# Third mixer's inverse in blocks of 32x32 and 64x64 at its two last levels, and its first products by pairs of heads

## The reference

```python
def _rwkv_scan(seqs, s0):
    # S_t = S_(t-1) diag(w_t) - (S_(t-1) kk_t) (kk_t * a_t)^T + v_t k_t^T,  y_t = S_t r_t
    def step(s, inp):
        rt, lwt, kt, vt, kkt, at = inp
        sa = jnp.einsum('bhvk,bhk->bhv', s, kkt)
        s = (s * jnp.exp(lwt)[:, :, None, :] - sa[..., None] * (kkt * at)[:, :, None, :]
             + vt[..., None] * kt[:, :, None, :])
        return s, jnp.einsum('bhvk,bhk->bhv', s, rt)
```

## Time and profile before

| | |
|---|---|
| runs of the kernel | 2309.73 us median of 3 (2306.72 to 2310.21) |
| the profiled execution | 2299.72 us, its span 2298.2 us |
| TensorE busy | 2160.4 us, 94% of the span |
| VectorE, ScalarE, GpSimd busy | 46%, 26%, 20% |
| granted clock of TensorE, mean | 0.972 of full speed |
| the chain that ended last | TensorE 82%, VectorE 6%, ScalarE 4%, DMA 3% |

### The profile page before, as it was taken

One profiled execution on the slowest core, in us unless ns is written; L12 is line 12 of the kernel. 1 busy time (PEld: TensorE's weight loads), 2 busy tenths in 40 slices (PEclk: granted clock), 3 DMA queues, 4 the chain that ended last, 5 costly groups with the idle time before them and its releaser, 6 DMA issues.

```text
span 2298.2 us, 33450 instructions
## 1 busy us (share of the span) xinstructions
PE 2160.4 (94%) x13459; PEld 2058.7 (90%) x13459; DVE 1054.4 (46%) x1540; ACT 604.8 (26%) x799; POOL 459.4 (20%) x463
## 2 busy tenths in 40 slices
PE   5998998899999897999999999999999999999995
PEld 3997887899999786899999999999999999999994
DVE  4051332467575445443433478642222235656654
ACT  3331221523232143112221243010000013333342
POOL 1122112444454331110000276210000010000012
PEclk9999998999999898999999999999999999999997
DMA  4122123412222240110101475131111224111112
GB/s 157 37 57 61 56 68 70 176 57 61 69 77 62 76 165 29 38 47 20 37 19 37 161 254 187 46 114 44 46 46 46 93 106 165 46 46 37 46 46 84
DMA packets 48563, 177.31 MB, mean 77 GB/s; under 512 B 6401, under 2 KB 6753, under 8 KB 48241
## 3 DMA queue, kind: packets, MB, share of 16 engines
q1 hardware_dynamic: 23040, 85.65, 12.1%
q0 software_dynamic: 17648, 61.31, 7.7%
q10 hardware_dynamic: 7808, 29.41, 3.3%
HBM read 128.84 MB, written 47.51 MB: 77 GB/s over the span
## 4 chain that ended last, share of the span: by engine, by line
PE 82%; DVE 6%; ACT 4%; DMA 3%; issue 2%; POOL 1%; DVEq 0%; SPq 0%; ACTq 0%; POOLq 0%
PE PS L463 25%; PE PS L623 20%; PE PS L1422 15%; PE PS L1384 2%; PE PS L1116 2%; PE PS L1295 2%; PE PS L1291 2%; PE PS L1283 2%; PE PS L1128 1%; DMA RING<-in_w_all 1%; PE PS L983 1%; PE PS L1249 1%; DVE AR L2059 1%; PE PS L1257 1%; POOL RING_parts L458 1%
## 5 line engine op out<-in xcount | busy, mean ns | idle before, releaser
L463 PE MATMUL PS<-HT_parts,WHIA_parts 128*128 128x352 f32 (+1 forms) x1440 | 510.4, 354 | 35.5 <-POOL RING_parts L458 20.0
L463 PE MATMUL PS<-OT_parts,WHIA_parts 128*128 128x352 f32 (+1 forms) x1440 | 477.6, 332 | 0.0
L463 PE MATMUL PS<-HT_parts,RING_parts 128*128 128x352 f32 (+1 forms) x1440 | 476.3, 331 | 0.0
L463 PEld LDWEIGHTS PS<-HT_parts,WHIA_parts 128*128 128x128 f32 x1440 | 280.1, 195 | 50.3 <-POOL RING_parts L458 21.4
L458 POOL TENSOR_TENSOR RING_parts<-RING,WHIA_parts 128x1024 fp32r<-128x1024 f32 x60 | 156.2, 2604 | 809.9 <-ACT WHIA_parts L453 809.9
L463 PEld LDWEIGHTS PS<-OT_parts,WHIA_parts 128*128 128x128 f32 x1440 | 279.4, 194 | 3.7 <-issue 0.2
L463 PEld LDWEIGHTS PS<-HT_parts,RING_parts 128*128 128x128 f32 x1440 | 278.8, 194 | 0.0
L1422 PE MATMUL PS<-MIXHI_parts,CF_parts 128*128 128x352 f32 x768 | 250.5, 326 | 3.4 <-DVEq L2571 2.9
L623 PE MATMUL PS<-HT_parts,CF_parts 128*128 128x352 f32 x768 | 249.7, 325 | 0.9 <-ACT AR L590 0.9
L1422 PE MATMUL PS<-MIXHI_parts,RING_parts 128*128 128x352 f32 x768 | 249.6, 325 | 0.0
L623 PE MATMUL PS<-HT_parts,RING_parts 128*128 128x352 f32 x768 | 248.4, 323 | 0.0
(11 more groups left out here) (394 smaller groups left out, 3607.2 us busy)
## 6 DMA issues: line engine op xcount, KB each, us to landing
RING<-in_w_all SPq DMA_DIRECT2D x132, 512.0 KB, 3.3
AR<-gates POOLq DMA_DIRECT2D x32, 528.0 KB, 4.0
proj<-AR ACTq DMA_DIRECT2D x18, 537.0 KB, 5.0
AR<-proj POOLq DMA_DIRECT2D x18, 537.0 KB, 8.3
gates<-CF ACTq DMA_DIRECT2D x16, 528.0 KB, 5.1
gates<-AR ACTq DMA_DIRECT2D x16, 528.0 KB, 5.1
AR<-in_xT SPq DMA_DIRECT2D x8, 537.0 KB, 14.3
AR<-in_xT POOLq DMA_DIRECT2D x8, 528.0 KB, 5.8
```

What stands on the lines that cost most here:

```text
L463: last = e.matmul(out, a_[:, u, k, :], b_[:, k, t], start=first and i == 0, stop=end and i == 2)
```

## The change

At the levels with `lh` of 32 and 64 (5 and 6, in full tiles only) each group multiplies only the blocks that the select lets through: at level 5 two products of 32x32 for each head, with 32 moving columns, at level 6 one of 64x64 with 64. `firsts` and `seconds` are the two halves of each block of twice `lh`; the weights, the moving rows and the result's partitions are taken from these. A `sem_inc` on a semaphore that nobody waits for stands between the waits and the products of a small group. The first products are written in another order: for each pair of heads, product by product, the two halves of the partitions by turns.

```diff
@@ -1266,34 +1266,58 @@
 
                 e.wait_ge(S("rw_copied"), n + 1)
                 e.wait_ge(S("rw_pre"), n + 1)
-                for h in range(4):
-                    r, g = slice(64 * (h % 2), 64 * (h % 2) + 64), h // 2
-
-                    ab = rc[r, g:g + 3:2, 0:w]
-                    e.matmul(PS(h % 2, g * 2 * w, (g + 1) * 2 * w)[0:w], rc[r, 6 + g, 0:w], ab, start=True, stop=True)
-                    e.matmul(PS(2 + h % 2, g * 2 * w, (g + 1) * 2 * w)[0:w], rc[r, 4 + g, 0:w], ab, start=True, stop=True)
-                    last = e.matmul(PS(4 + h % 2, g * w, g * w + w)[0:w], rc[r, g, 0:w], rc[r, 6 + g, 0:w], start=True, stop=True)
+                for g in range(2):
+                    for k in range(3):
+                        for b in range(2):
+                            r = slice(64 * b, 64 * b + 64)
+                            if k < 2:
+                                e.matmul(PS(2 * k + b, g * 2 * w, (g + 1) * 2 * w)[0:w], rc[r, 6 - 2 * k + g, 0:w],
+                                         rc[r, g:g + 3:2, 0:w], start=True, stop=True)
+                            else:
+                                last = e.matmul(PS(4 + b, g * w, g * w + w)[0:w], rc[r, g, 0:w], rc[r, 6 + g, 0:w],
+                                                start=True, stop=True)
                 last.then_inc(S("rw_s"), 1)
                 steps(gate, 8 if last_tile else 7)
                 for l in range(1, nlev):
 
                     lh, m = levels[l], w // 2
                     e.wait_ge(S("rw_t"), t0 + (2 if l == 1 else rw_ti(l - 1)))
-                    for h in range(4):
-                        last = e.matmul(PS(4, h * m, h * m + m)[0:w], pb[0:w, 2 * h * w:2 * h * w + w],
-                                        half(ti[0:w, h * w:h * w + w], lh, False), start=True, stop=True)
+                    firsts, seconds = ([slice(j, j + lh) for j in range(o, w, 2 * lh)] for o in (0, lh))
+                    small = lh >= 32
+                    if small:
+                        e.sem_inc(S("select_turn"), 1)
+                        for h in range(4):
+                            for j, (f, s) in enumerate(zip(firsts, seconds)):
+                                last = e.matmul(PS(4, h * m + j * lh, h * m + j * lh + lh)[s], pb[f, 2 * h * w + s.start:2 * h * w + s.stop],
+                                                ti[f, h * w + f.start:h * w + f.stop], start=True, stop=True)
+                    else:
+                        for h in range(4):
+                            last = e.matmul(PS(4, h * m, h * m + m)[0:w], pb[0:w, 2 * h * w:2 * h * w + w],
+                                            half(ti[0:w, h * w:h * w + w], lh, False), start=True, stop=True)
                     last.then_inc(S("rw_m"), 1)
                     steps(gate, 6 if last_tile else 1)
                     e.wait_ge(S("rw_m1"), n * 6 + l)
                     e.wait_ge(S("rw_t"), t0 + rw_tt(l - 1, False))
+                    if small:
+                        e.sem_inc(S("select_turn"), 1)
                     if l < nlev - 1:
                         for h in range(4):
-                            last = e.matmul(PS(1, h * m, h * m + m)[0:w], tt[0:w, h * w:h * w + w],
-                                            half(m1[0:w, h * w:h * w + w], lh, False), start=True, stop=True)
+                            if small:
+                                for j, (f, s) in enumerate(zip(firsts, seconds)):
+                                    last = e.matmul(PS(1, h * m + j * lh, h * m + j * lh + lh)[s], tt[s, h * w + s.start:h * w + s.stop],
+                                                    m1[s, h * w + f.start:h * w + f.stop], start=True, stop=True)
+                            else:
+                                last = e.matmul(PS(1, h * m, h * m + m)[0:w], tt[0:w, h * w:h * w + w],
+                                                half(m1[0:w, h * w:h * w + w], lh, False), start=True, stop=True)
                         last.then_inc(S("rw_n"), 1)
                     for h in range(4):
-                        last = e.matmul(PS(0, h * m, h * m + m)[0:w], m1[0:w, h * w:h * w + w],
-                                        half(tt[0:w, h * w:h * w + w], lh, True), start=True, stop=True)
+                        if small:
+                            for j, (f, s) in enumerate(zip(firsts, seconds)):
+                                last = e.matmul(PS(0, h * m + j * lh, h * m + j * lh + lh)[f], m1[s, h * w + f.start:h * w + f.stop],
+                                                tt[s, h * w + s.start:h * w + s.stop], start=True, stop=True)
+                        else:
+                            last = e.matmul(PS(0, h * m, h * m + m)[0:w], m1[0:w, h * w:h * w + w],
+                                            half(tt[0:w, h * w:h * w + w], lh, True), start=True, stop=True)
                     last.then_inc(S("rw_n"), 1)
                     if l == 1 and not first:
                         back_to_rows(n - 1, P)
```

## The result

The changed kernel takes 2297.43 us (median of 8 runs), the kernel before beside it 2308.57 (8 runs): a ratio of 0.995, 95% interval 0.9930 to 0.9969, so faster by 0.5% or 11 us. I had forecast 2322, slower by 0.5%. The time lies inside the widest range given (2294 to 2338) but outside the forecast's own (2312 to 2338), at the place of the first rival (2294 to 2300, no or one fall of the clock).

What follows compares the result with a forecast made beforehand. TensorE's own work was taken to bound full tiles: 2309.7 us, less 15.4 of work saved, plus 27.5 for five clock falls, gave 2322 us. The forecast's own range was 2312 to 2338, the widest 2294 to 2338.

Steps and rivals of the forecast that it cites:

- the first rival: Clock stays at 2.4 GHz, with no or one fall in the tiles: 2294 to 2300 us, faster; chance 0.27.
- the levels: Smaller products at levels 5 and 6 of full tiles: gain of 1.4 us a tile after the semaphore cost.
- the increments: Four added semaphore increments on TensorE's queue at levels 5 and 6: cost 0.2 us a tile, between 0 and 0.4.
- the first products: Alternating halves at a tile's first products lets both heads start together: gain 0.5 us a full tile, 0.2 in the last.
- The stretch to keys: Level 5 to the state products (keys): 4.3 to 4.7 us a tile at full clock, against 5.93 before.
- my lower bound of 0.016: Cost in us of one 32-row level-5 pass if a head's two blocks run side by side; 0.024 was assumed.
- The wait before level 6: TensorE idle about 0.5 us a tile before level 6's first load, waiting for VectorE's select.
- those five: Five 48-row stretches before the change, two followed by a clock fall; the new stretch was judged worse: 5 of 8 tiles fall.
- The price of a fall: Half-speed clock from keys to state update and some fill: 5.5 us a fall, bounds 3.4 and 7.2; five cost 27.5.
- the second rival: Clock falls in two or three tiles: 2305 to 2311 us, no measurable change; chance 0.10.
- Only the order counts: Levels 5 and 6 gain nothing, only the first products' new order does: 2305.5 us; chance 0.02.
- small passes as dear as large ones: Each small pass at levels 5 and 6 costs 0.111 us like a large one: 2317 us, slower; chance 0.03.

Runs made afterwards that it cites:

- e2: Changed kernel with the old order of the first products, so only levels 5 and 6 are small: 2304.72 us, ratio 0.9997.
- e1: Kernel before with only the new order of the first products, levels with 128 rows: 2308.22 us, ratio 1.0011.
- e7: Changed kernel with all heads' first blocks of level 5 queued ahead of their second blocks: 2297.00 us, ratio 0.9963.
- e5: Changed kernel with two fill steps instead of one at each of levels 5 and 6, taken from the tile's end: 2288.64 us, ratio 0.9928.
- e6: Changed kernel without fill steps at levels 5 and 6, both moved to the tile's end: 2334.60 us, ratio 1.0118.
- e15: Changed kernel, unaltered, profiled once more: 2308.55 us.
- e14: Changed kernel with levels 3 and 4 small too, 1 and 2 left large, fill steps spread among the small levels: 2297.27 us, ratio 0.9948.
- e9: Kernel before with four fill steps moved from behind the last tile into its state products: 2311.89 us, ratio 1.0032.
- e11: Changed kernel with a fill step in level 5's wait for the select and four in the last tile's state products: 2288.99 us, ratio 0.9932.
- e12: Changed kernel with levels 1 to 4 of full tiles small too and a fill step in each wait of levels 1 to 5: 2329.81 us, ratio 1.0107.
- e13: Same products as e12, with the 24 fill steps a tile placed otherwise, by a table per level: 2269.32 us, ratio 0.9802.
- e18: e13 with one fill step each from level 2's third group and level 4 moved to the tile's end: 2285.51 us, ratio 0.9885.

## Why the prediction was wrong

**What held.** TensorE's own work bounds the tiles, and the work saved is 15 to 18 us by span times clock (15.4 said). Its parts were a little small: 1.62 us a tile for the levels (e2; 1.4 said, after 0.2 for the increments), 0.53 for the first products (e1; 0.5 said), which makes 17.5 in all; that 15.5 and 15.4 agree so closely is luck. The stretch to keys is 4.16 us (4.3 to 4.7 said), as a small pass costs nearer to my lower bound of 0.016 than to 0.024: the two blocks run side by side, which e7 shows by taking it away. The wait before level 6 is there, 4.6 us over eight tiles (0.5 a tile said). The Trainium skill (TensorEngine Tiling (Array Packing), Gotcha 1: PSUM Pressure) says that different row tiles cannot access one PSUM bank at the same time. The prediction put that at 0.5 us a tile. The trace doesn't show such a cost: the two blocks of level 5 write one bank (other partitions of it), their 16 passes take 0.37 us, and e7's order, which puts their products apart, takes 0.52.

**The step that failed** is "I take that as worse than those five and count a fall in 5 of the 8 tiles". The profiles show one and three. The comparison with the five stretches of 48-row products looked at rows and waits alone and counted the fill in between for little ("two fill steps are all that has 128"). e5 and e6 show that the count of falls goes with these steps: none of them gives eight falls, one a level gives one to three, two give none, the last at the same idle time as one. Of the two falls that the comparison rested on, only the one at 801.3 came with TensorE busy throughout (3.80 of 3.80 us); before the one at 367.8 it was busy for 4.12 of 4.70. That the mechanism exists and where it would strike ("near the end of level 6 or at keys") was right; the changed kernel lies just on the good side of it, e6 on the bad one.

**The price of a fall**, 5.5 us, fits the falls of e6 (10.2 us at half speed, 5.1) but not those of the changed kernel (6.8 us low, 3.2 longer, just under the lower bound of 3.4): the low clock began later, at keys, and lasted 3.4 us less. With five falls at 3.2 the sum would have been 2309.7 - 15.4 + 16 = 2310, no change, so it took both, the count and the price, to come out slower.

**The rivals.** The first was right for the median and, with one fall, for the profiled run; e15, with three falls and 2308.55 us, lies where the second rival put two or three (2305 to 2311). Over the runs the clock took back 4 to 8 us. The Trainium skill (TensorE: Matmul & The Clock Gate, HAM oscillation) ties the lower clock to idle gaps. e14 agrees, with a fall in an idle stretch of 3.7 us; e1's 17.1 us at 0.50 with TensorE busy throughout is a fall that it doesn't cover. "Only the order counts" fails on e1; small passes as dear as large ones fail on the 0.37 us of 16 passes.

**Not foreseen**: that a change can lose its gain at a place that it doesn't touch. e1 saves 4 us in the tiles, and its two profiled runs lose some 8.5 in the last tile's state products. Neither part alone is measurably faster, though each saves its work; the clock outside the part under study moves by as much as the gain. Where that comes from was only narrowed down, not settled: with fill among those products none of three profiles has it (e9 to e11).

## What to carry to other kernels

Forecast a change of TensorE's work in two sums, the work at 2.4 GHz and the clock, and read both from runs: span times clock told the parts' gains to some 2 us where the times told nothing. Where products get smaller, move full-size work in between them, first into the waits that the shorter groups leave open: with the same products and the same 24 fill steps a tile, their places alone made 2330 us (e12) or 2269 (e13). Judge a step's place by what the clock does, too: e18 took two steps from among the small groups, for shorter tiles at 2.4 GHz, and lost 16 us to e13.

## What was not expected of the hardware

Products in different row groups overlap closely. With two groups 16 passes took 0.37 us in the chain; with four groups, in e13, 32 passes took 0.38 us, 12 ns a pass (the chain again):

```profile
1121.68 0.38 PE PS L1298 x32
```

The idle stretches named "issue" in e12 to e14, up to 3.7 us long and in the midst of a group of products, were not there in the changed kernel's tiles. The page's row of the instruction queue has 48 packets and 0.79 MB for the changed kernel and this for e13, which has more and smaller products:

```profile
q8 instruction: 79, 1.29, 0.2%
```

That TensorE waits there for its instructions would fit, but no run tests it.
